# Hybrid attention by row tile: tile 0's jobs, projection, queries and expert choice before tile 1's jobs

## The reference, cut to what matters

```python
def hybrid_layer(x, positions, norm1_gain, w_in, ...):
    proj = rmsnorm(x, norm1_gain) @ w_in
    (a_q, a_kc, a_vc, a_ks, a_vs, a_kw, a_vw, a_gate, b_cq, b_ckv, b_kr) = jnp.split(proj, pts, axis=-1)
    o_a = nsa_mixer(...)      # 8 heads of 64: compressed, selected and window branch, gated
    o_b = mla_mixer(...)      # 8 heads, queries and keys of 96, values of 64
    mixed = jnp.concatenate([rmsnorm(o_a, out_gain_a), rmsnorm(o_b, out_gain_b)], axis=-1) @ w_out
    h = x + mixed
    return h + peer_ffn(rmsnorm(h, norm2_gain), peer_w_q, peer_sub_keys, peer_u, peer_v)

def peer_ffn(x, w_q, sub_keys, expert_u, expert_v):
    q = _rms((xt @ w_q).reshape(T, P_HEADS, P_KEY_DIM))          # 8 heads
    s1 = jnp.einsum('thd,hnd->thn', q[..., :half], sub_keys[:, 0])
    s2 = jnp.einsum('thd,hnd->thn', q[..., half:], sub_keys[:, 1])
    ...                                                          # top 16 of each, top 16 of the pairs
    a = jnp.einsum('cd,ckd->ck', xc, expert_u[ec])
    w = gc * jax.nn.gelu(a)
    return jnp.einsum('ck,ckd->cd', w, expert_v[ec])
```

## Time and profile before

| | us |
|---|---|
| median of 3 runs | 1463.73 (1460.67 to 1466.08) |
| profiled execution, its own time | 1461.87 |
| its span on the core | 1460.1 |
| hybrid attention's loop, first turned to last weighed | 716.7 to 759.8 |
| first gather issued | 789.75 |
| first gather of tile 1 issued | 828.0 |

### The profile page before, as it was taken

How to read it: one execution, slowest core, us unless ns; L and a number is a source line. 1 busy time by engine, 2 the same in 40 slices (tenths; PEclk the granted TensorE clock), 3 DMA queues, 4 the chain that set the end, 5 groups by cost and what they waited for, 6 DMA issues and landing times.

```text
span 1460.1 us, 19575 instructions
## 1 busy us (share of the span) xinstructions
PE 1323.1 (91%) x6461; PEld 934.2 (64%) x6461; DVE 944.3 (65%) x2283; ACT 549.5 (38%) x1131; POOL 358.4 (25%) x372
## 2 busy tenths in 40 slices
PE   8999999999999999999999789797887979788877
PEld 6988999988988999977875435343343535343333
DVE  4687554564557555585764777776767777776755
ACT  4563544444555444454662122222222212222221
POOL 0104000000000000012402454435434344345440
PEclk9999999999999999999999899899999999999999
DMA  9614665545315565463403999999999999999997
GB/s 360 261 58 113 226 196 172 195 151 231 116 55 174 176 191 183 167 235 123 174 1 124 420 420 421 420 421 422 422 421 422 422 422 422 421 422 422 421 421 306
DMA packets 97534, 406.84 MB, mean 279 GB/s; under 512 B 6955, under 2 KB 44524, under 8 KB 60748
## 3 DMA queue, kind: packets, MB, share of 16 engines
q0 software_dynamic: 39552, 276.60, 46.1%
q1 hardware_dynamic: 57932, 129.60, 25.9%
HBM read 404.84 MB, written 1.07 MB: 278 GB/s over the span
## 4 chain that ended last, share of the span: by engine, by line
PE 51%; DMA 22%; issue 13%; DVE 9%; POOL 2%; ACT 2%; DVEq 0%; POOLq 0%; SPq 0%; ACTq 0%
DMA arena_u<-in_peer_uv,prob 20%; PE ps L685 12%; PE ps L686 12%; PE ps L687 12%; PE ps L838 6%; DMA uv_gain<-in_peer_uv,prob 2%; PE ps L906 1%; DVE arena_u L2506 1%; PE ps L632 1%; PE ps L812 1%; PE ps L625 1%; PE ps L641 1%; DVE prob L2382 1%; DVE prob L2370 1%; PE ps L623 1%
## 5 line engine op out<-in xcount | busy, mean ns | idle before, releaser
L1860 DVE TENSOR_TENSOR w_low<-ring,w_high 128x1024 fp32r<-128x1024 f32 x140 | 165.2, 1221 | 151.3 <-ACT w_high L1222 150.8
L1222 ACT ACTIVATE w_high<-ring 128x1024 fp32r<-128x1024 f32 x140 | 140.7, 1052 | 171.8 <-PE ps L687 171.8
L838 PE MATMUL ps<-arena_u,sco 128*128 128x512 f32 x256 | 126.8, 648 | 36.1 <-ACT sco L1459 36.1
L685 PE MATMUL ps<-hT_high,w_high 128*128 128x256 f32 x512 | 145.0, 283 | 0.9 <-DVE hT_low L1853 0.9
L686 PE MATMUL ps<-hT_low,w_high 128*128 128x256 f32 x512 | 144.9, 283 | 0.0
L687 PE MATMUL ps<-hT_high,w_low 128*128 128x256 f32 x512 | 144.8, 283 | 0.0
L1471 ACT ACTIVATE prob<-prob 128x4 f32<-128x4 f32 (+2 forms) x67 | 13.8, 206 | 343.5 <-DVE prob L2506 343.5
L1459 ACT ACTIVATE sco<-const,prob 128x128 f32<-128x128 f32 x256 | 84.7, 392 | 155.1 <-DVE prob L2516 137.4
L1661 POOL TENSOR_SCALAR small<-small 128x1 f32<-128x1 f32 x8 | 4.3, 533 | 499.2 <-ACT arena_v L1254 499.2
L838 PEld LDWEIGHTS ps<-arena_u,sco 128*128 128x128 f32 x256 | 52.3, 208 | 102.7 <-issue 57.0
L838 PE MATMUL ps<-arena_v,sco 128*128 128x512 f32 x256 | 117.7, 592 | 0.0
(11 more groups left out here) (440 smaller groups left out, 2955.7 us busy)
## 6 DMA issues: line engine op xcount, KB each, us to landing
ring<-in_w_up SPq DMA_DIRECT2D x32, 1024.0 KB, 5.5
ring<-in_w_down SPq DMA_DIRECT2D x32, 1024.0 KB, 4.8
qkring<-in_qk_a SPq DMA_DIRECT2D x8, 1024.0 KB, 7.1
qkring<-in_qk_b SPq DMA_DIRECT2D x8, 1024.0 KB, 4.9
ring<-in_peer_wq SPq DMA_DIRECT2D x7, 1024.0 KB
ring<-in_w_in SPq DMA_DIRECT2D x8, 860.0 KB, 5.5
ring<-in_w_out_a SPq DMA_DIRECT2D x4, 1024.0 KB, 15.6
ring<-in_v_b SPq DMA_DIRECT2D x4, 1024.0 KB, 6.9
```

Source lines behind the costliest of these rows:

```text
L685: pe.matmul(dst, a[0], b[0], start=start, stop=False, skip_group_check=True)
L838: last = pe.matmul(ps[2 * t + n][:, :], diag[:, k % N_DIAG, :], slots[k][:, D + n * HALF:D + (n + 1) * HALF], start=False, stop=(final and ...
L1222: sc.activation(w_split[pair][0][:, part], ring[:, slot, part], ACT.Copy)\
L1860: ve.tensor_tensor(w_split[pair][1][:, part], ring[:, slot, part], w_split[pair][0][:, part].bitcast(F32), ALU.subtract)\
```

## The change

The units become 18 **jobs** (`N_JOBS`). Jobs 0 to 5 (`FIRST_JOBS`) are tile 0's, with four heads each, one block per head; jobs 6 to 17 are tile 1's, with two heads each and two blocks per head. A job has 512 columns. Its scores always go to banks 4 and 5, its turned probabilities to bank 2, and ACT alone copies these (`take_job`). Scores of the next job wait for the mask of the last one (`sco_ready`). The low-rank queries and keys are turned by tile too, and the low-rank heads of a job are scaled by one instruction.

In step 8 the first half of tile 0's projection is multiplied, in step 9 comes the rest of it, then tile 0's rows, first queries, scores, squares and `first_choice_begun` (the best eight); step 10 has `first_choice_ended`. Then tile 1's jobs go on. Steps 18 and 19 have the first half of tile 1's projection, and `last_rows` the rest. POOL issues gathers 0 to 3 when the first eight are named, 4 and 5 when all low-rank parts are turned, and the others behind the last weighed job; the slots are put in another order, and small buffers move. The first head's weights and dots of tile 0 stand on DVE within tile 1's last steps, and tile 1's choice stands nearly in one piece in `first_unit`.

```diff
@@ tensor @@
+                def job_scores(j):
+
+                    t = 0 if j < FIRST_JOBS else 1
+                    if j:
+                        pe.wait_ge(sem("sco_ready"), count.take("sco_ready", len(job_parts(j - 1))))
...
+                for step in range(2, N_JOBS + 2):
+                    j = step - 2
+                    if step == 9:
+                        turn_out(1, 0, 3)
...
+                        for n in range(2):
+                            out_products(0, n, n, 1)
+                        turn_rows(0, (3, 0))
+                        landed("first_wq")
+                        first_queries(0, (1, 3), lambda c: hT_first[:, c, :])
+                        pe.wait_ge(sem("pq_ready"), count.take("pq_ready", 4))
+                        first_scores(0, 0)
+                        first_squares(0, 3)
+                    turn_job(j)
+                    if step in (4, 5):
+                        wait_low_rank(2)
...
+                    if step < N_JOBS:
+                        job_scores(step)
...
+                    if step == 18:
+                        pe.wait_ge(sem("out_turned"), count.take("out_turned"))
+                        out_products(1, 0, 4, 0)
+                    if step == 19:
+                        out_products(1, 1, 5, 0)
+                    weigh_job(j)
@@ scalar @@
+                def take_job():
+                    sc.wait_ge(sem("probT_a_turned"), count.take("probT_a_turned"))
+                    sc.activation(job_probT, ps[2][:, :], ACT.Copy).then_inc(sem("probT_a"), 1)
@@ gpsimd @@
             def first_unit():
 
+                po.wait_ge(sem("c_out"), count.take("c_out", 2))
                 po.wait_ge(sem("experts_ready"), count.take("experts_ready"))
                 alone()
                 for k in range(4):
                     gather(0, k)
                 power(ms_out[:, 0:1], ms_in[:, 0:1], "ms_ready", "rms_ready")
+                po.wait_ge(sem("m_turned_a"), count.take("m_turned_a", 8))
+                for k in range(4, 6):
+                    gather(0, k)
+                half_rms(1)
+                count.skip("weighed", 2 * N_LAYER_UNITS)
+                po.wait_ge(sem("weighed"), count.take("weighed", N_JOBS))
+                gather(0, 6)
+                half_rms(3)
+                gather(0, 7)
...
@@ vector @@
+                for step in range(2, N_JOBS + 2):
+                    j = step - 2
+                    if step == 9:
+                        add_out(0, 0)
+                        take_rows(0, 3)
+                        then(row_scale(0))
+                        first_choice_begun()
+                    job_share(j)
+                    if step < N_JOBS:
+                        job_bias(step)
...
+                    finish_job(j)
...
+                    if step == 10:
+                        first_query_rms(0)
+                        first_choice_ended()
...
+                ve.sem_inc(sem("norm_due"), 1)
+                dot(0, 0)
+                dot(0, 1)
+                out_scale(1, 1)
+                dot(0, 2)
+                dot(0, 3)
+                dot(0, 4)
+                add_out(1, 4)
+                take_rows(1, 7)
+                gates_in(0)
+                dot(0, 5)
+                row_scale(1).then_inc(sem("rows_scaled"), 1)
+                dot(0, 6)
+                weights_of(0, 0, 4)
+                first_query_rms(1)
```

More of the change, by code:

```diff
@@ L2578, in peer @@
             def peer():
[L2579 to L2593 removed]
+                first_unit()
                 unit(1)
```

497 lines of the change are left out of this document (281 added, 216 removed).

## The result

The changed kernel takes 1484.7 us (median of four runs, 1482.7 to 1486.9) where the kernel before takes 1462.3 in the same comparison: a ratio of 1.015, 95% interval 1.0124 to 1.0176. It is 22 us slower. The prediction said slower, by 10.3 us.

The account below looks back on a forecast made before the run. The full DMA pipe bounds it: attention 781.7 + 3.9 + 8.0 + 11.3 + 2.5 = 807.4, 34.0 to tile 1's names, 1.0 + 1.8 to restart at 844.2, 10.3 after 833.9; forecast 1474 us, range 1469 to 1479.

Parts of the forecast that it names:

- one full pipe: Second half: expert gathers and query weights fill the DMA engines, 263 x 2.49 = 655 us.
- The early gathers run dry: Before tile 1's gathers: tile 0's early ones are only 16 of 256; if the pipe empties before tile 1's names, the gain is lost.
- The hand-overs: Between attention jobs: turning, copy by ACT and weighing leave PE idle 11.3 us in steps 2 to 8 and 10 to 19.
- clock term: Attention loop: PE's clock falls after waits, 1.8 us for the 5.6 us wait, 0.7 for smaller ones, 2.5 us together.
- PE work of 65.0: Attention loop: PE's own work, 41.8 us as before plus output products and tile 0's rows, queries and scores, 65.0 us.
- the waits of step 9: Tile 0's projection, rows, queries and choice in one piece: hand-overs leave PE waiting 3.9 us.
- the choice's 8.0: Tile 0's choice on DVE: PE waits 2.4 us behind its first part and 5.6 behind its second, 8.0 us.
- Rival 3: Whole loop: clock falls throughout, mean 0.85, PE's 65 us become 76, 9 us more than forecast, 1483; chance 0.08.
- from the first turned probabilities (716.73): Start of the attention loop: the moment at which the kernel before begins it; PE alone would end at 781.7.
- The tail, "34.0 us": From attention's end to tile 1's names: 22.7 us up to the choice and 11.3 for it, 34.0 us.
- the last scale: Start of the tail: finish, squares, norm and scale until the last piece is turned, 3.6 us with two dots ahead on DVE.

Follow-up runs that it names:

- e7: Changed kernel with the edits of e1, e3 and e6 and constant turnings on PE (start, piece, step 10, tile 1's last outputs): ratio 1.0017 to the kernel before.
- e10: Changed kernel with constant turnings on PE in the waits its traces show, every wait left in: ratio 1.0068 to the kernel before.
- e1: Changed kernel with two bank pairs at the start, so job 0's and job 1's scores no longer share banks: 1481.6 us, ratio 1.012 to the kernel before.
- e5: Kernel before with one wait put in: unit 1's scores wait for DVE's four biases of unit 0: ratio 1.0027 to the kernel before.
- e6: Changed kernel with three reorderings behind its last job: POOL's and DVE's last scale and the queries' scale come earlier: ratio 1.0124 to the kernel before.
- e9: e7 with 14 and 5 further constant turnings on PE around tile 1's queries: ratio 0.9996 to the kernel before.
- e2: Changed kernel with constant turnings on PE, 18 before job 1's scores, others in tile 0's piece, choice and tail: ratio 1.0103 to the kernel before.
- e11: e9 with 4 more turnings ahead of the weighings of steps 10 to 12 and 19 for 15 ahead of step 10's scores: ratio 1.0002 to the kernel before.
- e12: e11 with DVE's dots of experts 7 and 8 and weights of experts 4 to 7 moved behind tile 1's names: ratio 0.9999 to the kernel before.
- e3: Changed kernel with the second part of tile 0's choice moved from step 10 to the start of step 18: ratio 1.0114 to the kernel before.

## Why the prediction was wrong

**Right.** The second half is one full pipe, and what counts is when it can go on with tile 1's gathers: 626.0 to 626.6 us from that gather to the end in nine traces. The direction. The early gathers run dry. The hand-overs: e7's loop, with full clock and without the second part of the choice, lasts 82.5 us from its start to the last weighing; with the 6.0 us of waiting that this part causes at full clock (e10) it is 88.5, with the 5.6 I had given it 88.1. The forecast without its clock term is 807.4 - 2.5 - 716.7 = 88.2. So the PE work of 65.0, the waits of step 9 of 3.9, the choice's 8.0 and the hand-overs' 11.3 are right in their sum. e10, with the choice in place, says the same: its loop lasts 92.5 us; from the scores issued in step 12 to the third turned job behind them it needs 12.5 us (783.35 to 795.82) where e7 needs 8.4 (776.48 to 784.88), and without these 4.1 us of half clock it is 88.4. This 88.4 is put together from two traces; no run had the choice in place and the clock up throughout. The choice's waits are 2.4 and 6.0 there, forecast 2.4 and 5.6.

**Mis-sized: the clock, "2.5 us".** The changed kernel's loop lasts 97.9 us, against 88.4 at full clock: the clock costs 9.5 there (5.4 came back in e10, the other 4.1 are the comparison with e7), 1.5 at the start (12.7 to 11.2, e10) and 2.6 in the tail (38.5 to 35.9). That is 13.6 in place of 2.5. I took the price of a wait from one row of the second half, where the clock was back after 8.82 us, and charged the small waits of steps 2 to 8 with almost nothing. Here it falls more often and stays longer. Behind the 2.46 us of waiting it is at half until 718.3; behind the waits of 0.78, 0.18 and 0.81 us at the loop's start from 724.7 to 734.8; and behind those of 2.28 and 3.72 us in the choice from 779 to 800. The wait of 2.46 us was in no term at all. Rival 3 had this mechanism with a chance of 0.08 and gave 1483, less than 2 us from the result. It put the loop's mean clock at 0.85, and it is 0.83 (722.4 to 820.3); that its time fits so well is in part luck, since it had neither the start nor the tail. I had named for it the rule of the Trainium skill, "TensorE: Matmul & The Clock Gate", section "HAM oscillation — how this bites in real kernels". Its way, read as a loss in every step with waits, did not come: in the changed kernel the steps from 735 to 747 have waits of 0.45 and 0.57 us at full clock, and 747 to 765 one of 0.78 and one of 0.40 at 1.00. I set the rival aside because the rows of before showed 1.00 from 716 to 790. They showed it for a PE without long waits (95% busy in the loop, 1.38 us the longest behind it), and the change takes that away.

**Missed: the loop's start.** The prediction lets the loop run "from the first turned probabilities (716.73)" as before. But the change gives jobs 0 and 1 one bank pair, and so puts a wait ahead of the loop. I had named "one bank pair" for the steps and not for the start. e1 and e5 show it: 1.1 us of the wait itself (11.2 with the clock up, 10.1 before) and the 1.5 of clock.

**The tail, "34.0 us".** With the gather's 1.0 it is 35.0 to the first gather; measured 38.5. At full clock it is 35.9 (e10). 2.6 of the 3.5 us are the clock and are counted above; the 0.9 left lie in the last scale, which waits for POOL's gather and two dots (forecast 3.6 us, measured 4.5, 820.26 to 824.74; e6 takes 1.1 off).

```profile
824.74 1.11 PE L918 MATMUL ps<-const,nat 128*128 128x128 f32 x4 [3.44 <-DVE nat L2425]
```

Sum: 10.3 + 1.1 (start) + 11.1 (clock, 13.6 less 2.5) + 0.9 (tail) = 23.4. Measured 21.9 to 22. The difference of 1.5 lies behind the restart: from there to the end it is 626.2 us in before (833.9 to 1460.1) and 624.6 in the changed kernel (860.5 to 1485.1). Part of it is how these two moments are read. By the bytes moved, 357 GB/s in 790 to 806 put the queue's start at 792.4 and the end of the 17 blocks at 834.8, and 369 GB/s in 860 to 865 put the restart at 860.6. That leaves 625.3 and 624.5; the 0.8 between them stay open.

## What to carry to other kernels

A long loop that is moved or cut anew does not keep its start: look at which buffers its first two rounds share and what waits for them. If PE was busy throughout and the change opens waits of even 1 to 3 us in dense work, price each not by its length but by the stretch at half clock behind it: ten microseconds and more here, of which one cost 3.8 us (e9). Dummy turnings in the waits gave back 9.5 of 22 us by the traces (e10), and no stage grew longer by them; half of that came from 18 turnings in a single wait (e2). And an early start of a transfer queue is worth only what is left of it when the queue next runs empty.

## What the runs showed of the hardware

- The clock falls with less waiting than I took for needed. In e1 PE was busy 14.63 of the 16 us from 700 to 716, with waits of 0.38 and 0.63 us near its end, and waits of 0.79, 0.18 and 0.81 us followed; the next group ran at half (1.86 us for what takes 1.10). With 12 turnings in two of these waits (e7, e9, e11, e12) it did not fall. Nor did it in e2, which has waits of 0.35, 0.78, 0.18 and 0.81 us in the same place, none of them filled; which sum or order of waits decides is open. The Trainium skill, "TensorE: Matmul & The Clock Gate", section "A second HAM failure mode: psum-queue depth-cycling", says that short idle times between groups of products can be enough for it. The trace of e1 agrees; that of e2 shows that such waits do not always do it.
- A fall is partly chance: e7 and e9 run the same instructions with the same waits of 0.64 and 0.56 us at 772, and one fell. Tile 0's queries, behind the same waits, ran at half clock in the changed kernel (5.44 us) and at full clock in e3 (3.81).
- PE can stay at half clock for 10 us while it works without a pause: in e1 from 720.7 to 731.0 it was busy all 10.3 us at a mean clock of 0.51, in the changed kernel from 790 to 800 for 9.97 of 10 us at 0.50. The 20 us from 780 to 800 are two such stretches with the wait of 3.72 us between them.
- Ahead of the loop, executions of one and the same program differ by up to 5 us, with the clock 0.98 and 0.94 in the stretches where others have 1.00. Differences below 0.3% have to be read between fixed points of two traces; the medians of the runs did not settle them.
